# Reordering the router tails, the expert gathers and three smaller places of a hybrid decoder step

## The reference

```
layer 0:  x += [causal pooling mixer | mLSTM matrix memory](norm(x)) @ w_out
          x += hmoe(norm(x))
layer 1:  x += glu(gelu(S5 scan(norm(x))) @ w_glu)
          x += hmoe(norm(x))
y = norm(x)

hmoe: 4 groups of 8 experts; top 1 group, then the top 2 experts in it, per token
      y[token] = sum over its 2 experts of weight * (silu(x@gate) * (x@up)) @ down
mLSTM, per chunk of 128 positions and head:
      S = (q k^T) * W,   num = S v + w_inter * C q,   C' = decay * C + (v * wg)^T k
S5:   h[t] = lam * h[t-1] + B u[t];   y = Re(C h) + D u     (64 groups of 16 channels)
```

## Time and profile before

| what | value |
|---|---|
| median of 3 runs | 1107.02 us (1106.66 to 1113.74) |
| the profiled execution | 1109.26 us, its span 1107.5 us |
| mean granted TensorE clock | 0.954 of 2.4 GHz |
| busy: PE, DVE, ACT, POOL | 948.7, 425.5, 182.8, 347.6 us |
| moved by DMA | 292.39 MB, 264 GB/s over the span |

### The profile page before, as it was taken

How to read it: one execution, slowest core, us unless ns; L and a number is a source line. 1 busy time by engine, 2 the same in 40 slices (tenths; PEclk the granted TensorE clock), 3 DMA queues, 4 the chain that set the end, 5 groups by cost and what they waited for, 6 DMA issues and landing times.

```text
span 1107.5 us, 15831 instructions
## 1 busy us (share of the span) xinstructions
PE 948.7 (86%) x5716; PEld 578.0 (52%) x5716; DVE 425.5 (38%) x945; ACT 182.8 (17%) x353; POOL 347.6 (31%) x613
## 2 busy tenths in 40 slices
PE   3999979899897878888687479999989999777776
PEld 2788869645554434444344456444456555444342
DVE  5301144767752223132227873003365322221216
ACT  5311021222210000000016421102351000000003
POOL 1278900184247666656641000000011122011100
PEclk9999989999799999899999879999998999999999
DMA  7126850650669999999983773904036999999965
GB/s 253 39 77 227 305 227 1 253 181 20 230 252 402 424 422 427 398 395 393 402 341 145 81 87 101 425 21 168 23 132 262 419 425 423 423 426 423 424 278 207
DMA packets 53600, 292.39 MB, mean 264 GB/s; under 512 B 11633, under 2 KB 22001, under 8 KB 34071
## 3 DMA queue, kind: packets, MB, share of 16 engines
q1 hardware_dynamic: 41607, 270.29, 62.9%
q0 software_dynamic: 8640, 16.03, 3.9%
q10 hardware_dynamic: 3296, 5.31, 1.7%
HBM read 270.47 MB, written 36.80 MB: 277 GB/s over the span
## 4 chain that ended last, share of the span: by engine, by line
PE 55%; DMA 29%; DVE 7%; SPq 4%; issue 3%; POOL 1%; ACT 1%; POOLq 0%; DVEq 0%; ACTq 0%
DMA arena<-in_w_gu 18%; PE ps L733 13%; PE ps L857 10%; PE ps L1001 9%; PE ps L1196 5%; DMA arena<-in_w_down 4%; PE ps L991 3%; SPq L564 2%; DMA arena<-scratch_hd,idx_now 2%; PE ps L928 2%; PE ps L887 2%; DVE arena L1592 1%; DMA arena<-scratch_kp 1%; PE ps L1153 1%; PE ps L1149 1%
## 5 line engine op out<-in xcount | busy, mean ns | idle before, releaser
L1001 PE MATMUL ps<-arena 128*64 128x256 f32 x2048 | 239.0, 389 | 57.6 <-DMA arena<-in_w_gu 57.6
L1001 PEld LDWEIGHTS ps<-arena 128*64 128x64 f32 x2048 | 147.8, 140 | 149.5 <-DMA arena<-in_w_gu 55.2
L2343 POOL TENSOR_TENSOR arena<-arena 128x256 f32<-128x256 f32 (+3 forms) x192 | 132.6, 690 | 41.7 <-POOL arena L2343 41.4
L2244 POOL TENSOR_TENSOR arena<-arena 128x32 f32<-128x32 f32 (+5 forms) x202 | 93.5, 463 | 159.7 <-DMA arena<-in_s_d 79.2
L733 PE MATMUL ps<-arena 128*128 128x260 f32 x640 | 142.0, 383 | 0.0
L991 PE MATMUL ps<-arena 128*64 128x512 f32 x512 | 120.5, 613 | 13.4 <-DMA arena<-in_w_down 12.8
L733 PEld LDWEIGHTS ps<-arena 128*128 128x128 f32 x640 | 121.4, 191 | 18.8 <-issue 0.4
L857 PE MATMUL ps<-arena 128*128 128x512 f32 x256 | 115.8, 603 | 3.9 <-DVE arena L1756 3.7
L1975 DVE TENSOR_TENSOR arena<-arena,ps 128x128 f32<-128x128 f32 x64 | 18.4, 288 | 261.1 <-ACT arena L1446 261.1
L1446 ACT ACTIVATE arena<-ps 128x128 f32<-128x128 f32 x64 | 17.8, 278 | 470.3 <-PE ps L1001 470.3
L1592 DVE TENSOR_TENSOR arena<-arena 128x32 f32<-128x32 f32 (+18 forms) x125 | 70.7, 565 | 35.6 <-DMA arena<-scratch_rows 21.7
(11 more groups left out here) (225 smaller groups left out, 980.9 us busy)
## 6 DMA issues: line engine op xcount, KB each, us to landing
arena<-in_w_gu SPq DMA_DIRECT2D x64, 2048.0 KB, 13.3
arena<-in_w_down SPq DMA_DIRECT2D x64, 1024.0 KB, 14.0
arena<-in_w_in SPq DMA_DIRECT2D x10, 1024.0 KB, 6.0
scratch_yd<-arena SPq DMA_DIRECT2D x2, 4160.0 KB, 18.6
arena<-scratch_yd SPq DMA_DIRECT2D x16, 512.0 KB, 7.4
arena<-in_w_out SPq DMA_DIRECT2D x1, 4096.0 KB, 12.2
scratch_hd<-arena ACTq DMA_DIRECT2D x8, 512.0 KB
arena<-in_w_glu SPq DMA_DIRECT2D x2, 2048.0 KB, 7.8
```

Source lines behind the costliest of these rows:

```text
L1001: mm = pe.matmul(ps[CAP * f:CAP * f + CAP, 2 + s, 0:256], XT[l][:, kc, CAP * s:CAP * s + CAP], WGU[l][i][s][:, kc, 256 * f:256 * f + 256], ...
L2244: step(g_.tensor_tensor(out, a, b, op))
L2343: g_.tensor_tensor(o, x, y, f).then_inc(sem("matrix_steps"), 1)
```

## The change

Seven edits of order; no arithmetic changes.

1. Start: SP issues x tile 0, the norm weights, the constants, then the other x tiles.
2. ACT: z14 ahead of all sixteen exponentials, z15 behind them. DVE: the three products on `ks` and `n0s` move behind chunk 0's key-value copies.
3. Router, PE: `first_rows` of the first four tiles stand right behind logits 4, each waiting for its own `HELD`; then position 4, `total`, list 0 of tiles 0 and 1, the first rows of the last tile, list 0 of tiles 2 to 4, transposes. DVE takes the largest count before the softmax.
4. List 1 moves from the end of the router to behind the first expert's gate and up product (`weight_lists`).
5. POOL gathers two pairs ahead: gather 1 and 2 before the wait for the third count of `lists_l`, then gather p+2 in pair p.
6. S5: `driven(7)` ahead of `columns(0)`, also in the ring's list of jobs.
7. PE's code: in layer 0 the first two pairs are written out ahead of the loop, in layer 1 the first twelve stand in a row instead of a loop of two times six.

```diff
-    j += [(("y", 0), "act"), (("zs", 7), "dve"), (("y", 1), "act")]
+    j += [(("zs", 7), "dve"), (("y", 0), "act"), (("y", 1), "act")]
...
-            load(place(CONST_AT, CONSTS), T["const"], "consts")
             for i in range(TILES):
                 load(X[:, i, :], every_fourth(T["x_prompt"], i), f"x_in_{i}")
+                if i == 0:
+                    load(GB, T["norms"][0], "norm_in")
+                    load(place(CONST_AT, CONSTS), T["const"], "consts")
...
-                for k in range(4):
-                    pe.wait_ge(sem("ranked"), 5 * l + k + 1)
-                    list_part(0, k)
-                position(4)
...
-                pe.wait_ge(sem("first_held"), 5 * l + 4)
                 for k in range(4):
+                    pe.wait_ge(sem("first_held"), 5 * l + k + 1)
                     for b in range(2):
                         first_rows(k, b)
+                position(4)
+                pe.wait_ge(sem("softmax_args"), l + 1)
+                done(pe.matmul(total_slot(l), ones, both, start=True, stop=True), "total", 0)
+                pe.wait_ge(sem("ranked"), 5 * l + 4)
+                for k in range(2):
+                    list_part(l, 0, k)
                 pe.wait_ge(sem("first_held"), 5 * l + 5)
                 for b in range(2):
                     first_rows(4, b).then_inc(sem("first_rows"), 1)
-                mm = list_part(0, 4)
+                for k in range(2, 5):
+                    mm = list_part(l, 0, k)
                 mm.then_inc(sem(f"list_done_{l}"), 1)
...
+            def weight_lists(l):
                 pe.wait_ge(sem("weighted"), l + 1)
                 for k in range(5):
-                    mm = list_part(1, k)
+                    mm = list_part(l, 1, k)
                 mm.then_inc(sem(f"list_done_{l}"), 1)
...
                             mm.then_inc(sem(f"gu_done_{l}"), 1)
+                            if isinstance(r, int) and isinstance(p, int) and p + s == 0:
+                                weight_lists(l)
...
-                        with pe.Fori(0, EP // 2 - 1) as k:
+                        for half in range(2):
+                            pair(half, half, 0, half)
+                        with pe.Fori(1, EP // 2 - 1) as k:
...
             for q in (4, 5, 6):
                 driven(q)
+            driven(7)
             columns(0)
-            driven(7)
...
+            z_out(14, Zv[:, 2])
             for h in range(H):
-                if h % 2 == 0:
-                    z_out(14 + h // 2, Zv[:, 2 + h // 2])
...
+            z_out(15, Zv[:, 3])
...
-            dve.wait_ge(sem("gate_exps"), 3)
-            tt(ks, ks, spread(SM[:, 4:8], P), ALU.mult)
-            tt(n0s, n0s, spread(SM[:, 0:4], P), ALU.mult)
-            tt(n0s, n0s, ks, ALU.add)
...
                     gather(1, 1)
+                    gather(2, 0)
                     pool.wait_ge(sem(f"lists_{l}"), 3 * r + 3)
...
-                    with pool.Fori(0, EP // 2 - 1) as k:
+                    with pool.Fori(0, EP // 2 - 2) as k:
                         for p, half in ((2 * k + 1, 1), (2 * k + 2, 0)):
-                            gather(p + 1, 1 - half)
+                            gather(p + 2, half)
                             scatter(p - 1, 1 - half)
                             build(p, half)
```

41 lines of the change are left out of this document (24 added, 17 removed).

## The result

| | before | after |
|---|---|---|
| median of 5 runs each, same chip | 1108.33 us (1106.66 to 1113.74) | 1117.78 us (1113.03 to 1120.47) |
| the profiled execution, its span | 1109.26, 1107.5 us | 1119.35, 1117.5 us |
| mean granted clock of TensorE | 0.954 | 0.934 |

The account below looks back on a forecast made before the run. No one engine bounds the span; DMA is full in both expert stages at about 425 GB/s. Terms 0 - 3.1 - 3.1 + 0.5 - 2.2 - 0.7 = -8.6 give 1100.7 us profiled, 1098.4 median; range 1089 to 1107.

Parts of the forecast that it names:

- start: Front, DVE's first scale: the wait for norms is exchanged for one for the tile; 0, ends -1.2 and +0.5 us.
- matrix memory: First key-value product: -3.1 us from starting sooner, -3.1 from the clock staying high, the latter with ends 0 and -3.1.
- layer 0 from the router on (B and C): Router 0's first product to S5's first `driven`: +0.5 us with the router's -2.1 in it, ends -4.5 and +3.7.
- S5 (D): First `driven` to router 1's first product: states ready earlier -4.7, filters' half 0 late +2.5, sum -2.2 us.
- layer 1 (E and F): Router 1's first product to the span's end: first gate and up moves -1.9, DMA hole of 1.2; -0.7 us.
- router tail: Both routers: clock rises under the moved first rows; first expert starts 2.1 us sooner in layer 0, 1.9 in layer 1.
- The position's place: Router 0: position behind sixteen passes ending at 302.8; position and counts end at 303.3, DVE's rank and held rows at 305.8.
- List 1: Layer 0's first pairs: `WL` 4.0 us later, down product at 327.9 instead of 323.96, POOL's build 0 ends 4.0 later.
- the stream gives it back: Layer 0's pairs: the DMA stream decides, +0.5 us, not POOL's chain, +2.4 at pair 2; POOL's shorter pairs catch up.
- The case priced at +5.0: S5 filters: two issuers together get only 106 GB/s, half 0 has 53 and ends 9.7 us late, +5.0 us.
- The written-out pairs: PE's code in the expert layers: no gaps at the loops' turns, so writing pairs out is priced at 0.
- the fourth: Rival, both routers: first rows wholly at the low clock, 13.7 us for 16 passes; +6.4, 1113.4 us, chance 0.05.

Follow-up runs that it names:

- a2: Changed kernel with the router's order of before in both layers, lists, first rows, position and counts placed as before; 1103.78 us, ratio 0.9966.
- a4: Changed kernel with 13 extra wide products, results unused, added in each router's tail; 1125.48 us, ratio 1.0152.
- b2: Changed kernel with list 1 at the router's end and the last position behind two tiles' row products instead of four; 1107.37 us, ratio 0.9991.
- c2: b2 with 6 wide products, results unused, added in layer 1's router tail alone; 1106.67 us, ratio 0.9985.
- a1: Changed kernel with list 1 alone moved back to the router's end, in both layers; 1112.03 us, ratio 1.0036.
- d1: Changed kernel with DVE making the selection rows of two tiles ahead of pair 0 and of three behind it; 1115.57 us, ratio 1.0052.
- b1: Kernel before with the edits of the start's loads and the matrix memory alone; 1104.02 us, ratio 0.9958.
- b3: a2 with SP and ACT issuing the second half of the filters only when the first has landed; 1100.08 us, ratio 0.9928.

## Why the prediction was wrong

By its own terms, in us of the profiled span:

| term | forecast | measured |
|---|---|---|
| start | 0 | -0.8 |
| matrix memory | -6.2 | -4.2 |
| layer 0 from the router on (B and C) | +0.5 | +8.4 |
| S5 (D) | -2.2 | +0.9 |
| layer 1 (E and F) | -0.7 | +5.7 |
| sum | -8.6 | +10.0 |

- **The step that failed is the router tail.** The prediction let the clock rise under the moved first rows, which it did, and then priced everything behind them at the high clock: last rows 1.7 us, twelve list passes 1.5, first expert 3.7. They took 3.78, 2.88 and 6.60. It had weighed whether the wide products would start slowly, and not whether the clock would fall again behind them. So the first expert started 0.4 us later, counted from the logits, instead of 2.1 sooner, and the down product, forecast 16.0 us behind that start, came 19.2 behind it. Before, the wide products had stood last, right ahead of the transposes and experts, and the clock was still high there. a2 shows that the order costs, a4 that the low clock makes the expert slow, b2 against c2 what the clock alone is worth, and the twelve tails against thirteen that it goes with the order.
- **The position's place** was in the sum and is not what made it fail. From the end of the logits to the last tile's rows the prediction had 12.4 us (293.4 to 305.8, with the position behind sixteen passes and DVE's 2.5 us behind it), and it took 11.8. (Its further terms add up to 311.7 for the expert's start, not 311.9, which changes nothing.) But it took the order's price as given. The 4.24 us idle on DVE are what the order costs there, and b2, with the position behind eight passes, was 4.7 us faster than a1.
- **List 1.** The chain from `WL` over the selection rows to the down product, and from `WL` over POOL's builds, was right link by link. It forecast +3.9 for the down product, and +9.6 was measured. Of the 5.7 us above, 2.5 stand ahead of the first expert's start and 3.2 behind it, 2.9 of them in that expert's own products at the low clock. PE was to wait for POOL at the first build; it didn't, because DVE's rows were later still, and d1 shows POOL's wait right behind. At pair 2 it did, with the 3.84 us. All of it came some 5 us later than forecast, since `WL` did (ready at 319.1 in an execution that was 5 us ahead, against 318.6). PE's waits for POOL's pieces lasted to the end of pair 5 (0.42 us there) and add up to 8.8 us, 2.9 before; those for gathered tokens, 7.4 us before, are gone. What was priced too well is that the stream gives it back. Of the forecast's 3.4 us the trace shows 1.2 in C.
- **Layer 1** was put at -0.7 on the ground that there is no build. The clock's price is much the same in both layers (E +8.3). F was 2.7 us shorter; that the three buffers gave this back is argued, and a2's F, 2.4 longer than before, shows how far that stage scatters.
- **Matrix memory.** The hole, 2.36 against 2.3 forecast, and the 3.0 us were right; the clock's 3.1 gave 1.2. The term's end of 0 for the clock would have been nearer. b1 has 5.7 us in A and 4.4 at the median for both edits, against 6.2.
- **Start 0** was right at its place (12.51 against 12.40 us). The 0.8 us came in the first 32 passes of 260 columns behind it, which took 9.17 us instead of 10.09 (8.86 in b1) with the clock rising earlier; whether the edit did that is open.
- **S5.** The states' part was right (no wait for them). The filters' half 0 was complete 6.4 us later, counted from the first `driven`, where 2.5 were forecast: 0.8 of it ahead of the first issue, 5.6 in the loading. That two queues move more than one, as read from the earlier trace rows, holds, but both rates were too high: 163 GB/s is that one window, the whole of half 1 before ran at 151, and beside half 0 the two together got 129, of which half 0 had 61 and not 82. The case priced at +5.0, 106 for both, didn't come. The Trainium skill's rule in "DMA: Bandwidth & Descriptors" (Issuing engines are not separate DMA queues) is that issuing from a second engine saves only the time of issuing. The 139 to 173 GB/s of two queues against 90 to 113 of one disagree with it for these loads, but half 0 still lost by the company. b3, which loads the halves in turn, wins 3.7 us by the medians.
- **The written-out pairs** show no stall, as priced.

Of the rivals the fourth had the place, the sign and nearly the size (1113.4), but another mechanism: it wanted the moved rows slow throughout, and 16 took 8.9 us and not 13.7. That its number came near is luck. The chance of 0.05 for a slower kernel was too small: the clock fell again behind the moved rows in all thirteen tails.

## What to carry to other kernels

In this kernel the wide products ahead of the experts kept TensorE's clock high for them, in twelve tails of twelve. Before moving such products forward, ask what will stand in their place, and price everything up to the next wide work at both levels. Before moving a long run of products ahead of a short one, look up which engine waits for the short one and for how long (here DVE, 4.24 us). When an early issue of the second half of a load competes with the first half, which alone is waited for, let it wait for the first to land.

## What the runs showed that was not expected

- One program, two clocks: 5.7 us between two executions of the same stage (b2 and c2), 5.1 of them in the tail. PE was busy without a gap when the clock fell in both.
- Keeping the clock up by added wide products works (1.00 over 28 us in layer 0 of a4) and costs more than it gives.
- Of DVE's ten selection rows the five of L1604 take 0.50 to 0.75 us in layer 0, where POOL works beside them, and 0.28 or 0.29 in the same place of layer 1, where POOL builds nothing. Of the five of L1607 only the first differs, 0.79 against 0.35. All ten take 5.6 us in the one and 3.5 in the other. No run changed POOL's part alone, so its share in this is argued:

```profile
321.01 0.79 DVE L1607 SCALAR_TENSOR_TENSOR arena<-arena 128x128 f32<-128x128 f32 x1
321.84 0.75 DVE L1604 TENSOR_SCALAR arena<-arena 128x128 f32<-128x128 f32 x1
...
866.47 0.35 DVE L1607 SCALAR_TENSOR_TENSOR arena<-arena 128x128 f32<-128x128 f32 x1
866.86 0.28 DVE L1604 TENSOR_SCALAR arena<-arena 128x128 f32<-128x128 f32 x1
```

- With a second issuing queue the filters load at 139 to 173 GB/s, with one at 90 to 113, and yet the second queue delays the half that is waited for. Why one queue alone gets so little is open; no run changed the sizes or the layout.
